# A second queue for the modulation tiles, and a new order of work in the state stage of a two-block network

## The reference

```
def modulate(x, g, shift, scale):
    return rmsnorm(x, g) * (1.0 + scale) + shift
shift, scale, gate = split(silu(c) @ ada_w + ada_b, 3)      # c is one vector of 1024

def s5_mixer(h, w_in, lam_re, lam_im, log_dt, b_re, b_im, c_re, c_im, d_skip, w_glu, w_out):
    u = h @ w_in
    # 64 groups of 16 channels drive a 64-dim complex diagonal state:
    #   x_t = lam_bar * x_{t-1} + B_bar u_t,   y_t = Re(C x_t) + d_skip * u_t
    y = gelu(y)
    y = y * sigmoid(y @ w_glu)
    return y @ w_out
h = h + gate * s5_mixer(modulate(h, ...), ...)
```

## Time and profile before

| | |
|---|---|
| median of 3 runs | 1838.74 us (1837.57 to 1838.76) |
| the profiled execution | 1840.31 us, span 1838.1 us |
| mean granted TensorE clock | 0.966 of full speed |
| PE busy | 1696.1 us, 92% of the span |
| DVE busy | 1072.7 us, 58% |
| ACT busy | 713.4 us, 39% |
| GpSimd busy | 68.7 us, 4% |
| HBM read | 192.71 MB |

### The profile page before, as it was taken

The page is one execution under the profiler, slowest core; times in us unless marked ns, Lnnn a source line. Parts: engine busy times, 40 slices in busy tenths (PEclk is TensorE's granted clock), DMA queues, the critical chain, the costliest instruction groups (busy, mean ns, idle before and its releaser), DMA issues.

```text
span 1838.1 us, 25591 instructions
## 1 busy us (share of the span) xinstructions
PE 1696.1 (92%) x9864; PEld 1342.0 (73%) x9864; DVE 1072.7 (58%) x1643; ACT 713.4 (39%) x1075; POOL 68.7 (4%) x122
## 2 busy tenths in 40 slices
PE   4969987999999989999979999999989999888996
PEld 2758766888888767777557888888777777765785
DVE  7799666666566664554545553455564564646443
ACT  4422323332233334444434332233436664445331
POOL 0040110000000000000000000000000000000000
PEclk9979998999999989999998999999989999999998
DMA  8331463334534344333111223321321211211231
GB/s 318 110 94 48 157 213 130 142 131 155 174 135 139 120 161 153 127 123 107 61 69 69 91 81 102 113 93 66 101 85 69 70 69 49 72 52 58 69 103 46
DMA packets 48484, 198.78 MB, mean 108 GB/s; under 512 B 8032, under 2 KB 12992, under 8 KB 34832
## 3 DMA queue, kind: packets, MB, share of 16 engines
q1 hardware_dynamic: 35728, 154.52, 24.3%
q0 software_dynamic: 12672, 43.10, 7.1%
HBM read 192.71 MB, written 4.23 MB: 107 GB/s over the span
## 4 chain that ended last, share of the span: by engine, by line
PE 76%; DVE 9%; issue 6%; ACT 5%; DMA 4%; SPq 1%; DVEq 0%; ACTq 0%; POOLq 0%
PE ps L474 23%; PE ps L475 22%; PE ps L476 22%; ACT w_hi L908 3%; DMA adaw<-in_ada_w 3%; DVE w_lo L1361 2%; PE ps L565 2%; PE ps L574 2%; PE ps L586 2%; PE ps L731 1%; DMA ada<-in_ada_k 1%; ACT pw L1011 1%; DVE adaw L1380 1%; PE ps L708 1%; PE ps L567 0%
## 5 line engine op out<-in xcount | busy, mean ns | idle before, releaser
L474 PE MATMUL ps<-xn_hi,w_lo 128*128 128x512 f32 x1264 | 511.5, 405 | 24.8 <-DVE xn_lo L1492 12.1
L475 PE MATMUL ps<-xn_lo,w_hi 128*128 128x512 f32 x1264 | 498.8, 395 | 0.0
L476 PE MATMUL ps<-xn_hi,w_hi 128*128 128x512 f32 x1264 | 498.7, 395 | 0.0
L1361 DVE TENSOR_TENSOR w_lo<-raw,w_hi 128x2048 fp32r<-128x2048 f32 (+1 forms) x145 | 312.2, 2153 | 232.9 <-ACT w_hi L908 232.7
L908 ACT ACTIVATE w_hi<-raw 128x2048 fp32r<-128x2048 f32 (+1 forms) x145 | 260.0, 1793 | 137.8 <-PE ps L476 135.8
L474 PEld LDWEIGHTS ps<-xn_hi,w_lo 128*128 128x128 f32 x1264 | 241.5, 191 | 83.8 <-issue 23.2
L476 PEld LDWEIGHTS ps<-xn_hi,w_hi 128*128 128x128 f32 x1264 | 241.0, 191 | 52.1
L475 PEld LDWEIGHTS ps<-xn_lo,w_hi 128*128 128x128 f32 x1264 | 241.7, 191 | 46.4
L474 PE MATMUL ps<-act_hi,w_lo 128*128 128x512 f32 x352 | 139.7, 397 | 2.6 <-DVE w_lo L1361 2.6
L476 PE MATMUL ps<-act_hi,w_hi 128*128 128x512 f32 x352 | 139.2, 396 | 0.0
L475 PE MATMUL ps<-act_lo,w_hi 128*128 128x512 f32 x352 | 139.2, 395 | 0.0
(11 more groups left out here) (367 smaller groups left out, 2416.5 us busy)
## 6 DMA issues: line engine op xcount, KB each, us to landing
raw<-in_weights SPq DMA_DIRECT2D x97, 1024.0 KB, 4.9
adaw<-in_ada_w POOLq DMA_DIRECT2D x80, 512.0 KB, 4.7
raw<-in_weights SPq DMA_DIRECT2D x16, 768.0 KB, 4.2
raw<-in_weights SPq DMA_DIRECT2D x16, 640.0 KB, 3.9
ada<-in_ada_k SPq DMA_DIRECT2D x8, 1024.0 KB, 18.0
fbias<-f_dram SPq DMA_DIRECT2D x16, 256.0 KB, 3.6
raw<-in_weights SPq DMA_DIRECT2D x8, 512.0 KB, 3.6
h<-in_xT SPq DMA_DIRECT2D x1, 2048.0 KB, 10.6
```

What stands on the lines that cost most here:

```text
L474: pe.matmul(bank, lo_w, hi_x, start=start, stop=False)
L475: pe.matmul(bank, hi_w, lo_x, start=False, stop=False)
L476: return pe.matmul(bank, hi_w, hi_x, start=False, stop=stop)
L1361: V.tensor_tensor(w_lo[:, b, 0:words], raw[:, b, 0:words], f32(w_hi[:, b, 0:words]), ALU.subtract).then_inc(split_lo, 1)
```

## The change

- GpSimd loads the eight modulation tiles `ada0`, as its first instructions; SP no longer does.
- `split` of chunk 0 moves on ACT ahead of the first turned copies, on DVE ahead of the modulation, out of the norm's first tile. `split` of chunk 2 moves on ACT ahead of turned copies 4 to 7.
- `turn_input(4..7)` run in one piece in the middle of the second product, the eight `input_kernel` in one piece after two of eight steps of the third.
- DVE takes the reciprocal of the first norm after all powers of B; the clearing of `ssq` moves behind the scan.
- `t1` and `t2` move to the places of `nt` and of `dd` with `ssq`, so DVE also waits for `u_saved[2]`, and `adaw` is free in the scan: GpSimd loads columns 16 and 17 when `rot` is done.
- Low parts 0 to 5 of the gelu output are subtracted by GpSimd (behind `xs_ready` of the next group); 6 and 7 stay on DVE, behind the loop. Columns 16 and 17 are reduced between them.
- In `s5_glu` the columns stand behind each evacuation (3, 3, 2, 0 of them), and 26, 27 ahead of the first of `s5_out`.
- GpSimd's cast of the constants and its clearing of `ssq2` move behind the scan.

```diff
-    t1, t2 = put("t1", ada_at, [P, 2, 4, NCK]), put("t2", ada_at + 4096, [P, 2, 4, NCK])
+    t1, t2 = put("t1", nt_at, [P, 2, 4, NCK]), put("t2", dd_at, [P, 2, 4, NCK])
...
     @block.sync
-        def load_ada(k):
-            sp.dma_start(ada0[k][:], ada_k[k * P:(k + 1) * P, :]).then_inc(ada0_in[k], 16)
...
-        load_ada(0)
...
-        for k in range(1, DT):
-            load_ada(k)
...
     @block.gpsimd
+        for k in range(DT):
+            pool.dma_start(ada0[k][:], ada_k[k * P:(k + 1) * P, :]).then_inc(ada0_in[k], 16)
         nc.gpsimd.memset(Bz[:], 0.0).then_inc(bz_clear, 1)
-        pool.wait_ge(in_late, 32)
-        nc.gpsimd.tensor_copy(cst16[:], cst[:]).then_inc(cst_ready, 1)
-        pool.wait_ge(cst_ready, 1)
-        nc.gpsimd.memset(ssq2[:], 0.0).then_inc(ssq2_ready, 1)
...
+        pool.wait_ge(rot_ready, 1)
+        for b in range(2):
+            pool.dma_start(adaw[:, b], ada_w[b]).then_inc(ada_in[b], 16)
         for i in range(2):
             pool.wait_ge(mt_in[i], 320 if i else 160)
         pool.dma_start(cvec[:], c.to_broadcast([P, D])).then_inc(in_c, 16)
-        pool.wait_ge(xs_ready, DT)
-        for b in range(2):
-            pool.dma_start(adaw[:, b], ada_w[b]).then_inc(ada_in[b], 16)
+        for m in range(DT - 2):
+            pool.wait_ge(gh_done, m + 1)
+            pool.wait_ge(xs_ready, m + 2)
+            nc.gpsimd.tensor_tensor(xn_lo[:, m], g32[:, m], f32(xn_hi[:, m]), ALU.subtract).then_inc(gl_done, 1)
+        pool.wait_ge(in_late, 32)
+        nc.gpsimd.tensor_copy(cst16[:], cst[:]).then_inc(cst_ready, 1)
+        pool.wait_ge(cst_ready, 1)
+        nc.gpsimd.memset(ssq2[:], 0.0).then_inc(ssq2_ready, 1)
...
     @block.tensor
-        product("s5_in", 0, 1, xn_hi, xn_lo, None, at_steps((3, 6, 9, 12), lambda n: turn_input(4 + n)))
-        product("s5_in", 1, 0, xn_hi, xn_lo, None, at_steps(tuple(range(8)), input_kernel))
+        product("s5_in", 0, 1, xn_hi, xn_lo, None, None, (0, 4))
+        for n in range(4, 8):
+            turn_input(n)
+        product("s5_in", 0, 1, xn_hi, xn_lo, None, None, (4, 8))
+        product("s5_in", 1, 0, xn_hi, xn_lo, None, None, (0, 2))
+        for i in range(8):
+            input_kernel(i)
+        product("s5_in", 1, 0, xn_hi, xn_lo, None, None, (2, 8))
...
     @block.scalar
+        split(0, 0)
         for n in range(2):
             turned_input(n)
         act.wait_ge(adr_done, 1)
         A(hn[:, 0], ps[:, 4], ACT.Copy).then_inc(adr_out, 1)
-        split(0, 0)
...
         input_out(0, 0, 0)
-        turned_input(4)
-        turned_input(5)
         split(1, 0)
-        turned_input(6)
-        turned_input(7)
+        for n in range(4, 8):
+            turned_input(n)
...
     @block.vector
-            if j == 1:
-                norm_stat("mix0")
         V.sem_inc(bw_ready, 1)
+        norm_stat("mix0")
         dve.wait_ge(cl0_ready, 1)
         power(1)
         power(2)
+        split(0, 0)
         dve.wait_ge(in_const, 32)
         first_modulation()
...
-        dve.wait_ge(u_saved[3], 64)
+        for n in (2, 3):
+            dve.wait_ge(u_saved[n], 64)
...
-            if m:
-                gelu_low(m - 1)
-            else:
+            if m == 0:
                 split(2, 1)
+        dve.wait_ge(gl_done, DT - 2)
+        gelu_low(DT - 2)
+        dve.wait_ge(xs_ready, DT)
+        V.memset(ssq[:], 0.0).then_inc(ssq_ready, 1)
+        dve.wait_ge(c_ready, 1)
+        ada(16, 2)
         gelu_low(DT - 1)
...
-            glu_and_ada(n // 2, n % 2, i)
+            glu(n // 2, n % 2, i)
+            ada(*((18, 3), (21, 3), (24, 2), (26, 0))[i])
...
         def out_and_ada(j, b, i):
+            if i == 0:
+                ada(26, 2)
             ada(28 + 3 * i, 1)
```

More of the change, by code:

```diff
@@ L660, in input_kernel @@
                 mm.then_inc(kt_done, 1)
[L662 to L669, removed]
         pe.wait_ge(part_out, 1)
@@ L1477, in norm_stat @@
                 V.memset(ssq2[:], 0.0).then_inc(ssq2_ready, 1)
-            if name != "out":
+            if name not in ("mix0", "out"):
                 V.memset(ssq[:], 0.0).then_inc(ssq_ready, 1)
@@ L1483, in norm_spread, with norm_tiles @@
             dve.wait_ge(rstd_out, NIDX[name] + 1)
-        def norm_tiles(name, src, scale, shift=None, hi=None, lo=None, dst=None, bank=7, behind_first=None):
+        def norm_tiles(name, src, scale, shift=None, hi=None, lo=None, dst=None, bank=7):
             n, x0 = dict(NORMS)[name], XTILE[name]
@@ L1500, in norm_tiles @@
                 V.scalar_tensor_tensor(to, src(m), scale(m), ps[:, bank], ALU.mult, ALU.mult).then_inc(norm_t, 1)
-                if m == 0 and behind_first:
-                    behind_first()
                 if hi is not None and m:
@@ L1687, in _ @@
         norm_spread("mix0")
-        norm_tiles("mix0", lambda m: h[:, m], lambda m: gain[:, 0, m:m + 1], lambda m: mod[:, 0, m:m + 1], xn_hi, xn_lo,
-                   behind_first=lambda: split(0, 0))
+        norm_tiles("mix0", lambda m: h[:, m], lambda m: gain[:, 0, m:m + 1], lambda m: mod[:, 0, m:m + 1], xn_hi, xn_lo)
         split(0, 1)
```

## The result

The changed kernel takes **1842.64 us** (median of 18 runs, 1841.46 to 1845.93); before took 1838.8 beside it (median of 18, 1836.29 to 1843.08). The ratio is 1.0021, 95% interval 1.0014 to 1.0028: slower by 2.6 to 5.1 us. The forecast was 1834.6; its rival *record by record* gave 1842.5. The profiled execution took 1843.87, with a span of 1842.2.

A forecast was written before the change was run, and what follows sets the result against it. TensorE, holding 76% of the chain, was taken as the main bound, though the chain was read in time order over the first 260 us. -0.3 - 1.3 + 0 - 2.5 = -4.1 us from 1838.74 gave 1834.6, range 1829 to 1843.

The forecast's parts named there:

- record by record: Rival at the start: queues alternate single records, x lands at 31.2, start 52.5 (+7.6); total 1842.5; chance 0.20.
- (a): Kernel start, modulation tiles on GpSimd's queue: first product matmul at 44.6, 0.3 us earlier; bounds -3.6 and +7.6.
- whole transfers in turn: Loads at the start: each queue gets one transfer in turn, so x lands at 16.2; the forecast's case, chance 0.45.
- The formula of (a): From x's landing to the first product matmul: 8.3 + 0.2 + 12.8 us; binding only for x later than 23.6.
- lands in good time: First weight chunk at the start: there early enough for ScalarE to split it before the turned copies; DVE done at 36.3.
- (b): First products, turns and input kernels in one piece: seven of eight changeovers saved, turns nothing; -1.3 us, bounds -0.6 and -2.
- (d): The scan: moving t1 and t2 and taking six low parts off DVE gains 0.
- PE binds: In the scan TensorE's period of 9.4 us against DVE's 9.3 sets the pace, so relieving DVE gains 0.
- (e): Columns of ada_w: two reduced within the scan, column 30 used near 252 instead of 253.92; -2.5 us, bounds 0 and -4.

The follow-up runs named there:

- x before the tiles: The changed kernel, but GpSimd waits until x has landed before issuing the eight modulation tiles (also called "x first"): 1833.93 us, ratio 0.9976.
- TensorE's list rearranged: The changed kernel with TensorE's products over modulation tiles 0 to 4 moved ahead of the square sums: 1841.17 us, ratio 1.0012.
- grouping alone: The kernel of before with only the turns 4 to 7 and the eight input kernels in one piece each: 1836.68 us, ratio 0.9988.

## Why the prediction was wrong, step by step

**The step that failed is (a), "whole transfers in turn".** I took x at 16.2 and the start at 44.6; x came at 32.66 and the start at 56.22. The bound "record by record" had x at 31.2 and the start at 52.5. I chose by the earlier trace rows, where in 215 to 218 us the column's queue moved 5 records against 110, and read it as no fair split by record. The same view of before, cut to 218 to 219 us:

```profile
q0 software_dynamic: 46, 0.19, 53.6%
q1 hardware_dynamic: 20, 0.13, 31.1%
```

The column, issued at 214.76, has all five records of the earlier trace rows in the last of those three microseconds, from 217.2 on; up to then its queue had none on the engines. When it had many, the weight load was running out (3 records in 219 to 221). I had averaged the microseconds before a queue's first record with those of two queues at work. The row spoke neither for nor against turns by record, and chances of 0.45 and 0.20 on it were the error. Why the first record took 2.4 us stays open: a column with no other load beside it (x before the tiles, issued at 244.35) had 20 records by 246. The kernel that undoes this one thing (x before the tiles, 1833.9) lands 0.7 us from the forecast of 1834.6, though partly by errors that cancel:

**The formula of (a)**, start = x + 21.3, was 2.3 short (x + 23.6): VectorE waited 1.92 for a modulation that I had put "at about 41" whatever x did. With TensorE's list rearranged it is x + 21.1.

**The chunk "lands in good time"** is right where it has a queue of its own (VectorE splits it at 48.80 without a wait) and not with the tiles ahead of it (37.13).

**(b), -1.3 with a bound of -2: the trace gives -4.0.** (7 x 0.2 makes 1.4; I carried it on as 1.3.) The kernels were mis-sized: one in a product sets it back by 0.56 (matmuls at 83.21, 83.89 and 84.23 in before, less two paces of 0.23), eight by 4.5; eight in one piece by 2.1 in all (86.24, 88.48, 88.82 in after); that is 2.4 where I had 1.4, as 16 short matmuls in a long row also take less by themselves, 0.24 for 0.36. The turns, given nothing, gain 1.0 (5.1 against 4.1). Of the rest, 0.6, the first product's slow matmuls are 0.4: its first 12 start within 4.50 us in before and 4.14 in after, and I can't place the last 0.2. They are slow because the granted clock is 0.50 of full speed behind the wait ahead of them (44.9 to 49.0 in before; the lower level, 1.2 of 2.4 GHz), and they are 0.43 apart instead of 0.23. How many there are changes from trace to trace: the 13th starts 4.73 behind the first in before, 5.25 with grouping alone and 2.84 with x first, where none is slow. Counted from the 49th matmul to the fifth chunk's split, grouping alone gains 3.6, as much as in after. VectorE's wait of 7.23 is gone, and its place before the fifth chunk holds 1.82 and 1.79, a little under the 4 foretold. Measured alone, the edit keeps only 1.3 to 2.2 of the time.

**(d), 0: between 0 and 1 us, -0.2 in after.** GpSimd's subtraction takes 1.28 to 1.30 us, within the bounds of 0.61 and 2.29, and nobody waits for it:

```profile
151.22 1.29 POOL L455 TENSOR_TENSOR xn_lo<-rot,xn_hi 128x512 fp32r<-128x512 f32 x1 [7.63 <-DVE XS L1772]
```

But "PE binds" was read at 173.7 to 183.1. In the scan's head VectorE binds; before, 133 to 143 us:

```profile
133.00:143.00 10.00, 9.27 (x197) 8.54 (x198) 9.90 (x18) 2.38 (x4) 0.00 (x0) 0.83 0.02 3
```

There the 0.4 us that a period is shorter can count; the working read only a later window. By the periods it should not be much: VectorE's with the low parts is 9.32, TensorE's 9.4, so that VectorE catches up. The rule of the Trainium skill, SBUF — State Buffer, section "SBUF: two separate sides", on GpSimd and VectorE excluding each other, is not put to the test by any run here: the subtraction above (151.22 to 152.51) lies beside VectorE's two products with a PSUM input (151.18 to 153.54), as the prediction had it, and the next one with two SBUF inputs starts at 153.57. The other five lie the same way. Giving the subtractions back to VectorE made no kernel faster.

**(e), -2.5 with bounds of 0 and -4: -5.0 in after**, 3.4 to 5.2 in all: from the first split of s5_glu to column 39 it takes 84.7 to 86.3 in the nine traces with the edit, 89.7 to 90.0 in the three without. The mechanism was right: in the variant with x first the last gating starts 29.25 behind the end of that split, as worked out, and h's first residual is level with before to 0.4. The size was not: I gave column 30 a landing of 4.6 us, near the median of all columns, and 1.9 us of gain (253.92 to 252; for the other 0.6 of the -2.5 the prediction has no working). Free of a weight load it lands in 3.7 in that variant:

```profile
244.35 0.53 POOL L465 DMA_DIRECT2D adaw<-in_ada_w  x1 [5.08 <-DVE mod L1376]
```

```profile
248.05 1.23 DVE L1376 CUSTOM_DVE_ANT_0 adaw<-adaw,cvec 128x1024 f32<-128x1024 f32 x1 [0.35 <-DMA adaw<-in_ada_w]
```

Relative to the first split it is used 3.4 earlier than before (49.9 against 53.4). The rest, 0.5 there and 1.4 in after, comes with the nine columns behind it, loads of which I had called unchanged.

In after (a)'s miss of 11.6 us outweighs what (b), (d) and (e) bring beyond forecast: 2.7, 0.2 and 2.5. That the sum ends at the rival's 1842.5 is luck in its size: that rival had +7.6 and -3.8, the trace has +11.3 and -9.2.

## What to carry to other kernels

A transfer put on a second queue is not beside the others for free: while both queues have work they take turns by record, so the queue with the longer records takes most of the bytes, and a latency-critical load in 2 KB rows behind it can take three times as long. Start such a load first and let the bulk wait for its landing, or keep both in one queue in the order of need; here the latter, with the weight chunk at the place where its split needs it, is 0.36% faster than before. And before a row is used as evidence about sharing, cut it finely enough to see that both queues are at work in it.

## What the runs showed of the hardware

- Two or three queues with work gave nearly equal numbers of records whatever their length: 511 and 504, 869 and 874, 309, 302 and 313.
- A queue can be alone for some microseconds though others have loads issued: with x on a queue of its own, 630 records were gone by 8 us, and the software queue's began at 6 instead of 2 to 3; in before, a column issued at 214.76 beside a weight load had its first record at 217.2.
- Software queue loads cut to rows of 2 KB left data records of 4 KB: 80 a load for 128 rows, 16 of them closing ones. x's 2 KB rows on the hardware queue stayed records of 2 KB.
- A column of 0.5 MB landed in 3.7 us with nothing else on the queues, and in 6.1 to 7.2 beside a whole weight load, around a median of 4.7.
- Short products in a long row are cheaper than in small groups: 16 of them between two large ones take 0.36, 128 in a row 1.92, or 0.24 for 16.
